# First tile's first query block multiplied by contraction block ahead of the second tile's last output half, with the second tile's gate and norm behind the first choice

## What is computed

```python
def block(xb):                                     # 128 tokens
    q = jnp.einsum('td,de->te', xb, w_q).reshape(PEER_BLOCK, PEER_HEADS, 2, PEER_QDIM // 2)
    s = jnp.einsum('thpk,pnk->thpn', q, sub_keys).astype(jnp.float32)
    s_top, i_top = lax.top_k(s, PEER_TOPK)
    cand = (s_top[:, :, 0, :, None] + s_top[:, :, 1, None, :]).reshape(PEER_BLOCK, PEER_HEADS, PEER_TOPK * PEER_TOPK)
    ...
    g_top, pos = lax.top_k(cand, PEER_TOPK)
    expert = jnp.take_along_axis(cand_idx, pos, axis=-1)
    g = jax.nn.softmax(g_top, axis=-1)
    u = jnp.take(peer_u, expert, axis=0)
    act = jax.nn.gelu(jnp.einsum('thkd,td->thk', u, xb).astype(jnp.float32), approximate=False)
    vv = jnp.take(peer_v, expert, axis=0)
    return jnp.einsum('thk,thkd->td', (g * act).astype(xb.dtype), vv)
```

## Time and profile before

| | |
|---|---|
| median of 3 runs | 2529.31 us (2526.57 to 2533.3) |
| profiled execution, span | 2524.7 us |
| mean granted TensorE clock | 0.913 of full speed |
| first gather of expert rows | 1097.54 us |
| DMA rate, mean over the span | 326 GB/s |

### The profile page before, as it was taken

How to read it: one execution, slowest core, us unless ns; L and a number is a source line. 1 busy time by engine, 2 the same in 40 slices (tenths; PEclk the granted TensorE clock), 3 DMA queues, 4 the chain that set the end, 5 groups by cost and what they waited for, 6 DMA issues and landing times.

```text
span 2524.7 us, 33890 instructions
## 1 busy us (share of the span) xinstructions
PE 2032.2 (80%) x12150; PEld 1384.9 (55%) x12150; DVE 1719.8 (68%) x3454; ACT 955.0 (38%) x2101; POOL 658.8 (26%) x631
## 2 busy tenths in 40 slices
PE   8999999999999999997665587777577778556555
PEld 7999899899989979874321123243122325211111
DVE  5687787768778867677588555558754757776544
ACT  4434533444544345432332224423223732322222
POOL 0000001000000100024445433344432335444442
PEclk9999999999999999999887798899788889887767
DMA  7545577674547763279999999999999999999998
GB/s 304 212 167 209 182 277 283 240 262 161 202 172 277 268 256 142 84 319 388 422 421 422 419 423 422 403 421 421 412 404 401 421 410 383 421 422 421 422 421 337
DMA packets 110947, 823.98 MB, mean 326 GB/s; under 512 B 14432, under 2 KB 15344, under 8 KB 31040
## 3 DMA queue, kind: packets, MB, share of 16 engines
q0 software_dynamic: 90000, 595.97, 57.8%
q1 hardware_dynamic: 20784, 225.89, 23.3%
HBM read 820.76 MB, written 1.05 MB: 326 GB/s over the span
## 4 chain that ended last, share of the span: by engine, by line
PE 47%; DMA 27%; DVE 11%; ACT 5%; issue 4%; POOL 2%; DVEq 2%; ACTq 1%; SPq 0%; POOLq 0%
DMA ring_b<-in_peer_uv,eidx 17%; PE pd L647 14%; PE pa L647 10%; PE pr L1269 9%; PE pr L647 7%; DMA wring<-in_peer_uv,eidx 6%; DVE wring_r L1971 2%; DVE ring_b L2672 2%; DMA ring_c<-in_peer_uv,eidx 1%; DVE wring L2672 1%; PE pa L1387 1%; ACT junk L1719 1%; POOL ring_b L1915 1%; PE pd L1292 1%; PE pa L1292 1%
## 5 line engine op out<-in xcount | busy, mean ns | idle before, releaser
L1269 PE MATMUL pr<-ring_b,junk 128*64 128x512 f32 x880 | 288.6, 765 | 156.5 <-ACT junk L1719 155.8
L1269 PE MATMUL pr<-wring,junk 128*64 128x512 f32 x840 | 269.4, 748 | 171.1 <-ACT junk L1719 170.6
L1915 POOL DMA_INDIRECT ring_b<-in_peer_uv,eidx x220 | 252.9, 1150 | 532.8 <-PE pr L1269 302.4
L2672 DVE CUSTOM_DVE_ANT_0 ring_b<-ring_b,hrow 128x1024 f32<-128x1024 f32 x220 | 267.9, 1224 | 180.9 <-DMA ring_b<-in_peer_uv,eidx 174.2
L2672 DVE CUSTOM_DVE_ANT_0 wring<-wring,hrow 128x1024 f32<-128x1024 f32 x210 | 255.4, 1223 | 187.8 <-DMA wring<-in_peer_uv,eidx 181.7
L1915 POOL DMA_INDIRECT wring<-in_peer_uv,eidx x210 | 247.8, 1180 | 332.6 <-PE pr L1269 277.3
L1709 ACT ACTIVATE gel<-dots 128x2 f32<-128x2 f32 x255 | 51.8, 203 | 654.4 <-DVE dots L2672 650.7
L1899 POOL DMA_DIRECT2D aring<-in_ada_rows x112 | 60.2, 538 | 840.9 <-DVE adal L2066 787.3
L1269 PEld LDWEIGHTS pr<-ring_b,junk 128*64 128x64 f32 x880 | 69.3, 165 | 350.8 <-ACT junk L1719 242.6
L1269 PEld LDWEIGHTS pr<-wring,junk 128*64 128x64 f32 x840 | 64.1, 159 | 345.6 <-ACT junk L1719 243.5
L1971 DVE TENSOR_TENSOR wring_r<-wring,wtop 128x2048 fp32r<-128x2048 f32 x76 | 171.7, 2261 | 54.7 <-ACT wtop L1431 52.4
(11 more groups left out here) (441 smaller groups left out, 4566.4 us busy)
## 6 DMA issues: line engine op xcount, KB each, us to landing
wring<-in_w_mix SPq DMA_DIRECT2D x38, 2048.0 KB, 8.8
aring<-in_ada_rows POOLq DMA_DIRECT2D x112, 512.0 KB, 5.1
wring<-in_w_ffn SPq DMA_DIRECT2D x22, 2048.0 KB, 8.3
wring<-in_w_lstm SPq DMA_DIRECT2D x12, 2048.0 KB, 7.7
wring<-in_w_stick SPq DMA_DIRECT2D x12, 2048.0 KB, 11.7
wring<-in_w_back SPq DMA_DIRECT2D x8, 2048.0 KB, 8.1
ring_c<-in_w_stick SPq DMA_DIRECT2D x5, 2048.0 KB, 12.1
wring<-in_w_back SPq DMA_DIRECT2D x4, 1536.0 KB, 6.9
```

What stands on the lines that cost most here:

```text
L1269: m = nc.tensor.matmul(pr[half][side, :], diag[:, p % DIAGS, :], row(p)[:, D + half * 512:D + (half + 1) * 512], start=p in FIRST_OF_SIDE, ...
L1915: pool.indirect_dma_start(out=row(q), out_offset=None, in_=ins["peer_uv"], in_offset=bass.IndirectOffsetOnAxis(ap=eidx[:, tt % NT, CHOSEN[ ...
L2672: m = nc.vector.tensor_tensor_reduce(out=row(q)[:, 0:D], in0=row(q)[:, 0:D], in1=hrow[:, q // PICKS % NT, SIDE[q], :], scale=1.0, scalar=0 ...
```

## The change

The orders of the engines change as follows; no arithmetic is added or left out.

- TensorE: piece 14 of tile 1 is cut after its fourth contraction block. Between its halves stands `queries(0, 0)`, now with the contraction block as the outer loop (`first_queries`): blocks 0 to 3 need the low half of the modulated tile, blocks 4 to 7 a new semaphore, `high_columns`. `keys(0, 0)` comes ahead of piece 15. `columns_of_tile(1)` moves from ahead of `keys(0, 0)` to behind `keys(0, 1)`.
- VectorE modulates column blocks 0 to 3 alone (`low_modulated`), ScalarE blocks 4 to 7 (`high_modulated`). Of tile 1's gate, VectorE does the first half before `choose(0, 0)`; the second half, the sum, the norm and the modulation stand behind it.
- ScalarE: `tile_squares(1)` moves behind `rows_back(0)`; the exponents of the first choice move ahead of the copy of `query(0, 1)`.
- GpSimd waits for both halves of tile 1's product before the first gather.
- `PLAN[0]`: 10 dots within the second choice and 10 behind it, instead of 13 and 7.

```diff
-PLAN = [counted(0, choice("part", 13, 1, sum(CHOICE_WORK) // 4) + [("between", 7)] + ...
+PLAN = [counted(0, choice("part", 10, 1, sum(CHOICE_WORK) // 4) + [("between", 10)] + ...
...
+                def first_queries():
+                    m = SLOTS_L
+                    pe.wait_ge(w_in_slot[place_of(m)], landed_b(m))
+                    b = bank_a()
+                    for k in range(KC):
+                        if k == 0:
+                            pe.wait_ge(thT_ready, 1)
+                        if k == FIRST_HALF:
+                            pe.wait_ge(high_columns, 1)
+                        for c in range(4):
+                            i = mm(b[:, c * P:(c + 1) * P], place(m)[:, k, c * P:(c + 1) * P], hT[:, k, 0:P],
+                                   k == 0 and c == 0, k == KC - 1 and c == 3)
+                    i.then_inc(pa_full, 1)
...
-                out_rows(pr[3], 1, 14)
+                out_rows(pr[3], 1, 14, range(FIRST_HALF))
+                settle()
+                first_queries()
+                out_rows(pr[3], 1, 14, range(FIRST_HALF, KC))
+                pe.wait_ge(experts_in, 32)
+                keys(0, 0)
                 out_rows(pr[3], 1, 15)
                 settle()
-                pe.wait_ge(thT_ready, 1)
-                queries(0, 0)
-                columns_of_tile(1)
-                pe.wait_ge(experts_in, 32)
-                keys(0, 0)
                 queries(0, 1)
                 rows_back(0)
                 keys(0, 1)
+                columns_of_tile(1)
                 pe.wait_ge(thT_ready, 2)
+                pe.wait_ge(high_columns, 2)
                 queries(1, 0)
...
+            def high_modulated(t):
+                u = DEPTH * D_UNITS + 4 + 4 + 4 + 2 + 2 * t + 1
+                act.wait_ge(pd_full, u + 1)
+                for i in range(4):
+                    c = FIRST_HALF + i
+                    m = nc.scalar.activation(hT[:, c, t * P:(t + 1) * P], pd[u % 2][:, i * P:(i + 1) * P], ACT.Identity,
+                                             scale=modA[:, 1, c:c + 1], bias=adac[:, 3 * KC + c:3 * KC + c + 1])
+                m.then_inc(pd_free, 1)
+                act.drain().then_inc(high_columns, 1)
...
             def experts_first():
-                for t in range(NT):
-                    tile_squares(t, mixed, True)
+                tile_squares(0, mixed, True)
+                high_modulated(0)
...
                 query(0, 0)
                 key(0, 0)
+                exponents(0, 0, *CHOICES[0][0][1:])
                 query(0, 1)
-                exponents(0, 0, *CHOICES[0][0][1:])
                 rows_back(0)
+                tile_squares(1, mixed, True)
                 key(0, 1)
+                high_modulated(1)
                 query(1, 0)
...
+            pool.wait_ge(late_rows, 2)
...
             tile_normed(0, 0, True)
+            low_modulated(0)
+            late_gated(0)
...
             choose(0, 0)
+            late_gated(1)
+            gated_sum(1, mixed)
+            tile_normed(1, 1, True)
+            low_modulated(1)
             choose(1, 0, spread_over(0, "part"))
```

More of the change, by code:

```diff
@@ L129, in counted @@
     return dict(out)
+FIRST_HALF = KC // 2
 QUERIES_BY = ((0, 0), (0, 1), (1, 0), (0, 2), (0, 3), (1, 2), (1, 1), (1, 3))
@@ L188 @@
 STICK_BEFORE = [0, len(STICK_GROUPS[0])]
-PLAN = [counted(0, choice("part", 13, 1, sum(CHOICE_WORK) // 4) + [("between", 7)] + choice("rest", 25) + [("late", 13)] + choice("choose", 50)),
+PLAN = [counted(0, choice("part", 10, 1, sum(CHOICE_WORK) // 4) + [("between", 10)] + choice("rest", 25) + [("late", 13)] + choice("choose", 50)),
         plan_of(0), plan_of(1), counted(0, [("first", 2)] + choice("late", 40))]
@@ L479, in build @@
         tss_ready, txn_ready, thT_ready = sem("tss_ready"), sem("txn_ready"), sem("thT_ready")
+        high_columns = sem("high_columns")
         mixed, experts_done, stick_done = sem("mixed"), sem("experts_done"), sem("stick_done")
@@ L1065, in keys, with out_rows @@
                     key_bank(lambda hp, cut: qp[t][:, hp, cut], q4)
-                def out_rows(b, t, m):
+                def out_rows(b, t, m, ks=range(KC)):
                     if t == 0:
@@ L1071, in out_rows @@
                     i = rows_product(b, m, tile_of(y_hi, t), tile_of(y_lo, t),
-                                     lambda k: k % 4 == 0 and pe.wait_ge(yT_ready, 2 * t + k // 4 + 1))
+                                     lambda k: k % 4 == 0 and pe.wait_ge(yT_ready, 2 * t + k // 4 + 1), ks)
+                    if KC - 1 not in ks:
+                        return
                     if t:
@@ L2557, in _, with low_modulated, late_gated @@
             gated_sum(0, mixed)
-            tile_normed(0, 0, True)
-            tile_modulated([(1, hT[:, :, 0:P])])
-            for half in range(2):
+            def low_modulated(t):
+                b = take()
+                nd[0] += 1
+                for c in range(FIRST_HALF):
+                    nc.vector.tensor_scalar(hT[:, c, t * P:(t + 1) * P], b[:, c * P:(c + 1) * P], modA[:, 1, c:c + 1], shift(1)[:, c:c + 1],
+                                            ALU.mult, ALU.add)
+                dve.drain()
+                dve.sem_inc(pd_free, 1)
+                dve.sem_inc(thT_ready, 1)
+            def late_gated(half):
                 c = slice(half * 512, (half + 1) * 512)
@@ L2563, in _ @@
                 nc.vector.tensor_tensor(xn[:, 1, c], pr[2 + half][:, :], grows[:, 0, c], ALU.mult)
-            gated_sum(1, mixed)
-            tile_normed(1, 1, True)
-            tile_modulated([(1, hT[:, :, P:SEQ])])
+            tile_normed(0, 0, True)
+            low_modulated(0)
+            late_gated(0)
             def parts(lists, n):
```

## The result

The changed kernel takes 2537.6 us in the median of six runs (2534.2 to 2542.0), the kernel before 2529.4: ratio 1.0034, 95% interval 1.0024 to 1.0044. That is slower by 8.2 us, just past the 0.3% that the prediction called measurable. The forecast was 2535.2 us and no change; the time lies in its range (2526 to 2541).

A forecast was written before the change was run, and what follows sets the result against it. Bound: the stream of gathers, with TensorE leading from 1140 to 1180 us. Span 2524.7 plus 4.8 (late second tile) plus 1.1 (clock) is 2530.6; runs lie 4.6 above, so 2535.2 us, called no change; range 2526 to 2541.

The forecast's parts named there:

- Part 1: Ahead of the gathers: query from about 1069.85, choice from 1080.25, first gather at 1092.3 us instead of 1097.54, 5.2 us earlier.
- Part 2: Second tile's sum, norm and transposes behind the first choice: `queries(1, 0)` starts at 1101.65 instead of 1096.85, 4.8 us later.
- Part 3: TensorE's clock drops behind idling around tile 1's transposes: 0.93 us lost there, 1.1 in all with the query.
- From nothing to the 1.74 us: Clock loss allowed for `queries(1, 0)`; upper end is what eight matmuls lost behind 5.70 us of idling.
- Part 4: Early gathers: head start spent by gather 8, later gathers 5.9 us later as TensorE frees places; plan number costs nothing.
- so little is lost: Gather 6 waits for `queries(1, 0)`, done at 1110.1; six gathers of 2.49 us last until about 1112.
- The sum: Whole kernel: 2524.7 of span plus 4.8 plus 1.1 gives 2530.6; runs lie 4.6 above the span, so 2535.2 us.
- (a): Rival: TensorE's lag is made up before the gathers need it, the head start stays; 2524.1 us, chance 0.12.
- (b): Rival: clock stays low through `queries(1, 0)`, 7.4 us becoming 14.8; 2542.4 us, chance 0.19.
- (c): Rival: ScalarE's table switch costs more than its row, twice the 1.28 us; 2536.5 us, chance 0.05.
- (d): Rival: first query slower or waiting for `high_columns`, first choice not earlier, tile 1 slips 5.2 us more; 2540.4, chance 0.04.
- its own signs of being wrong: Gather 28 coming at or before 1172 us, or full DMA windows from 1110 to 1125 us.

## Why the prediction came out as it did

**Part 1 (early first gather): right.** The first query starts at 1072.12 less 2.37, 1069.75 (1069.85 predicted); the first gather at 1092.25 (1092.3). The choice starts at 1080.27 (1080.25), by the first of these rows of VectorE, timeline of the changed kernel:

```profile
1082.64 0.49 DVE L2622 MAX8 top<-sc 128x8 f32<-128x128 f32 x2 [9.89 <-ACTq L1654]
...
1095.33 1.23 DVE L2396 TENSOR_TENSOR x<-x,xn 128x1024 f32<-128x1024 f32 x1
...
1101.54 0.75 DVE L2414 TENSOR_SCALAR xn<-x,rsx 128x1024 f32<-128x1024 f32 x1
```

**Part 2 (late second tile): right in kind, short by about 1 us.** By the two other rows the sum ends at 1094.19 (1094.2 predicted), the norm at 1099.92 instead of 1099.1. The step that failed is "four banks of rows back, one per 0.98 us: free at 1094.7": they are free at 1095.75, since the early gathers slow two of them. With both waits filled, this part stands alone: 5.97 us at the first product, where 4.8 was written. In the change itself `queries(1, 0)` starts 6.8 us late, of which 0.93 is the slow transposes.

**Part 3 (clock): the mechanism right, the size wrong, and this is the term that failed.** "From nothing to the 1.74 us", "I take 1.1 in all". In the profile the transposes lost 0.93 as predicted, but the queries 2.4 (9.81 for 7.41), then the products behind waits that were there all along 1.7 and 1.3: 6.4 us. Filling the waits gave back 6.3 at gather 28 and 7.1 in the medians. The working looked at the work behind the two new gaps alone. It left out that a clock price can fall due at later gaps, behind work that came through them at full clock in the kernel before; that it is the new gaps that bring this on is not shown, since 50 idle products without a gap did it too. Its bound from the nearest row was too low as well: eight matmuls that take 1.94 us at full clock can at most lose as much again, so the 1.74 that they lost was no upper end for a block of 7.4. In the change the granted clock is 0.50 from the start of the queries to 1110 us, 0.73 from there to 1112 and 1.00 behind it.

**Part 4: the waits right, the times carry the errors of parts 2 and 3.** Gather 6 waits for `queries(1, 0)` and gather 8 for the first product; the head start is spent; the number of the plan is worth nothing. But "so little is lost" at gather 6 fails: it is issued at 1114.3 (end of the queries predicted at 1110.1), and from 1112 to 1118 us of the changed kernel's span the DMA share is 0.15, 0.00 and 0.00 in steps of 2 us. Gather 8 comes at 1122.0 instead of 1118.7, and gather 28 at 1184.6 instead of "near 1178". That "each gather is issued when TensorE has freed its place, as before" holds for the waits and not for the clock behind them.

**The sum: two errors against each other.** With the measured terms it reads 2524.7 + 6.0 + 6.3 = 2537.0 of span. The prediction then added 4.6 for how the runs stood to the profiled span of the kernel before; the changed kernel needs 0.6. The terms were 6.4 us too small, the 4.6 was 4.0 too large, and that the forecast came within 2.4 us is luck. The trace of before was an execution 2.9 us below its median (4.6 less the 1.7 us around the span), and that was taken over to a kernel whose delay replaces the place where the luck seems to have been.

**The rivals.** (a), head start kept, fell: held back, the gathers end no later. (b), clock low through `queries(1, 0)`, decided from 1.9 us lost in the query: it lost 2.4, so its threshold was passed, but of 7.4 us at stake a third was lost, and 3.0 more later. The time lies between the forecast and (b)'s 2542.4. What spoke against it, "the clock returned within those eight matmuls", was misread: in the kernel before the granted clock is 0.50 from 1207.8 to 1209.5 and 0.50 from 1209.5 to 1211.4 us, over the whole of the 3.68 us, and 0.98 only behind it. So the 0.19 rested on a row that spoke for (b). The Trainium skill (TensorE: Matmul & The Clock Gate, What's actually happening) says that activity releases the clock and that the same kernel can catch it at another point from run to run. The traces agree with the first (1.97 becomes 1.09 behind idle products). The second is not seen: in three profiles of the change, one of them with the plan's number put back, the falls stand at the same places. It is across kernels that they move: behind the second wait of 1.96 us in the change, behind both with the first gap filled. (c), the table switch at twice its price, fell: 0.01 us lies between load and next operation, as in the kernel before. (d) fell with part 1. ScalarE's timeline of the changed kernel:

```profile
1099.22 1.28 ACT L1705 ACT_TABLE_LOAD   x1
1100.51 0.20 ACT L1705 ACTIVATE rsx<-ssx 128x1 f32<-128x1 f32 x1
```

By its own signs of being wrong the prediction was not wrong: gather 28 came after 1172, and from 1110 to 1130 us the DMA share is 0.59. The time is in its range. The side was not the one it favoured: it gave 0.73 to a change within 0.3% and 0.24 to a slower kernel, and the 8.2 us are 0.32%, with an interval (0.24 to 0.44%) that has the bound within it.

## What to carry to other kernels

When an edit opens a gap on TensorE ahead of a chain that TensorE leads, price the clock not only in the work behind the new gap but look at each gap that follows until the chain ends, since work that came through them at full clock may not when it is shifted. Try idle products in the new gaps: here 23 of them gave back 7.1 of 8.9 us. A head start for transfers is worth only what their buffers can hold: six gathers here, while the seventh waited for the engine that the same edit had delayed. Before a profile's own time is carried over, rebuild it from stretches that several profiles share; here one execution stood 3 us below its median, most likely in a place that the edit removes.

## What the runs showed of the hardware

- The same wait of 1.96 us on TensorE was followed by 3.22 or by 4.92 us for the same product, with the same work around it. With `queries(1, 0)` at 9.81 us the fall came at the second such wait, at 8.73 and 8.82 at the first and the second, at 7.38 (both waits filled) at none. But with 50 idle products and the queries at 7.31 it came at the second, so how slow the queries were doesn't decide it.
- The clock comes back late: behind waits of 4.56 and 1.68 us, with 1.97 us of transposes between them, it was at 0.50 through the first 4 us of the queries. Idle 128x128 products kept it up: 16 of them took 3.84 us of the first wait, and the transposes behind the 0.73 to 0.81 us that remained ran at 1.09.
- While the first gathers are issued, TensorE's rows back reach ScalarE later (0.72 and 0.98 us of wait instead of 0.32 and 0.28), which holding the gathers back took away. In the ten microseconds behind the first gather's issue, three kernels in the old order show "issue" waits of 1.3 to 2.3 us in all between matmuls that wait for nothing in the program; the profile of the kernel before and those of the two changed kernels with the gather held back show none over 0.3 us. Their cause is open.
